# Further blocks of a mixture-of-experts kernel at 64 rows: high and low halves side by side in one stationary operand, woven into the first block's work

## Chip, cores and metric

One NeuronCore of a Trainium2 chip runs the whole program in one launch. The metric is the time on the device in microseconds (us); three executions of the kernel before are given, and their median stands for it. "PE" is the matmul engine, "ACT" the scalar engine, "DVE" the vector engine, "POOL" the general engine that also issues the indirect DMAs, and "SP" the engine that issues the other DMAs.

## The reference, cut to what matters

A decoder layer: forgetting attention, a residual with layer norm, and then a mixture of experts with 64 routed experts and one shared one. The change is in the mixture of experts. With T = 1024 tokens of width 1024 and an inner width of 256:

```python
scores = jax.nn.sigmoid((xf @ w_router).astype(jnp.float32))
...
_, top_e = lax.top_k(jnp.where(exp_mask, sel, -jnp.inf), TOP_K)   # 8 of 64 experts for each token
...
h = jax.nn.silu(xb @ w_gate[e]) * (xb @ w_up[e])
yb = (h @ w_down[e]) * rw[:, None].astype(xb.dtype)
return acc.at[rows].add(yb), None
...
shared = (jax.nn.silu(xf @ ws_gate) * (xf @ ws_up)) @ ws_down
```

So each expert has a list of the tokens that chose it. Computed from the reference on its own inputs, the 64 lists have 101 to 159 tokens, 128 on average. 33 experts have 128 tokens or fewer; 31 have more, and none of them over 159. Those 31 are experts 2-4, 6, 7, 9, 10, 15, 17, 19, 20, 22-27, 30, 31, 33-37, 39, 42, 44, 49, 51, 53 and 63. They form 16 runs, so 16 of them follow an expert without surplus (or the start) and 15 follow another one with surplus.

## The kernel before

The program first computes the attention (eight pairs of heads), then the output projection, layer norm and routing, token tile by token tile. DVE computes for each (token, expert) pair a place in a table (`place`), and POOL writes the token numbers into the table in DRAM (`list_tokens`). The table has `TAB_BLOCKS` = 8 columns per expert, each a block of up to 128 tokens.

Then come the blocks. A block is up to 128 rows of tokens and one expert's weights. The eight blocks of the shared expert (`SH` = 8) come first; then `expert(e, par)` is called for e = 0 to 63 on each of the engines, most of it in a loop over pairs of experts. Every operand of a matmul is held as two float32r parts, high and low, and a product is three matmuls: high by high, high by low, and low by high.

On PE a block has these parts:

- `turn_rows`: eight transposes of 128x128 that bring the gathered rows (`x_rows`) into a PSUM tensor, from which ACT copies the high part (`xb_hi`) and DVE subtracts the low part (`xb_lo`);
- `gate_up`: 24 matmuls with 512 moving columns into `banks[0]`: 16 with the high rows (against `gu_hi` and `gu_lo`) and 8 with the low rows;
- ACT takes the silu (`sg`), DVE multiplies (`hh`), and `turn_h` transposes the result (two transposes), ACT and DVE split it into `ht_hi` and `ht_lo`;
- `down`: 12 matmuls of 512 columns into `k_ps`, 8 with `ht_hi` and 4 with `ht_lo`; ACT scales the result by the token's weight into `ys` (`scale_rows`), and POOL adds it to a sum in DRAM (`scatter_add`, an indirect DMA).

An expert has a first block of up to 128 rows, and `further[e]` further blocks of up to 128 rows more; on these inputs that is 0 or 1. The order on PE inside `expert(e)` is: turn h of the block before; gate and up of the first block; if there is a further block, turn its rows into `out_ps`; turn the next expert's rows into `q_ps`; down of the block before; and then, if there is a further block, turn h of the first block, gate and up of the further block, and down of the first block. The further block's own h and down follow in the next expert.

The weights of one expert are three matrices of 1 MB. SP loads them into two raw buffers, ACT copies the high part (`w_high`, `L1166`, four pieces for gate and up and two for down), and DVE subtracts the low part (`w_low`, `L1546`), while the previous set is used.

POOL goes through its list in this order in `expert(e)`: wait until DVE has read the weights' column of the block (`w_ok`), gather the rows of expert e + 2; if expert e + 1 has a further block, gather its rows (`x_rows` 2, 128 rows of 4352 bytes); then add the results of expert e - 1 to the sums. A gather is a copy of 128 indices (`L575`) and then the indirect DMA (`L578`); an addition is the same with `L585` and `L588`.

Of the kernel before, what the change touches and what calls it, by code (L numbers as in the profile page):

```python
# [5 lines left out]
P = 128  # L6
BANK = 512
# [12 lines left out]
VC = 256  # L20
# [36 lines left out]
TAB_BLOCKS = T // P  # L57
# [16 lines left out]
def build(nc, x, w_in, b_f, w_out, ln1_g, ln1_b, router, router_bias, w_gate, w_up, w_down, ws_gate, ws_up,  # L74
          ws_down, ln2_g, ln2_b, out):
    with ExitStack() as ctx:
# [31 lines left out]
        with ExitStack() as early:  # L108
# [38 lines left out]
            with ExitStack() as d:  # L147
# [47 lines left out]
                pos_b = sb("pos_b", [P, E], c=d)  # L195
                dest = sb("dest", [P, E], c=d)
# [10 lines left out]
        with ExitStack() as m:  # L207
# [4 lines left out]
            xb_hi = [sb(f"xb_hi{i}", [P, DC, P], F32R, c=m) for i in range(3)]  # L212
            xb_lo = [sb(f"xb_lo{i}", [P, DC, P], F32R, c=m) for i in range(3)]
# [5 lines left out]
            wcol = [sb(f"wcol{i}", [P, 1], c=m) for i in range(3)]  # L219
# [23 lines left out]
        for n in ("consts masks xt_ps xt_hi_ok xt_lo_ok wf_in wf_ok bf_in zt_ps zt_ok z_ps z_ok zabs_ok zexp_ok zlog_ok zmin_ok gate_ok"  # L243
                  " c_ps c_hi_ok c_lo_ok c_stored wv_hi_ok wv_lo_ok v_ps v_ok aug aug0 mx20"
# [4 lines left out]
                  " g_hi_ok g_lo_ok d_hi_ok d_lo_ok tab_in started gated turned rows_hi_ok rows_lo_ok silu_ok h_ok ht_ps ht_hi_ok"  # L249
                  " ht_lo_ok downed scaled w_ok x_in x_turned x_rows_hi_ok x_rows_lo_ok x_w_ok ax_ok ax_stored summed"  # L250
                  " stands g2_in std_ok var_ok f_part set_free f_sum f_var f_std f_step f_mv f_norm f_g f_out").split():
            S[n] = sem(n)
        tile_in = [sem(f"tile_in{t}") for t in range(TT)]
        wv_in = [sem(f"wv_in{i}") for i in range(2)]
# [5 lines left out]
        wo_in = [sem(f"wo_in{i}") for i in range(STAGES)]  # L260
# [16 lines left out]
        S["sidx_ok"] = sem("sidx_ok")  # L277

# [42 lines left out]
        def _(sp):  # L321
# [3 lines left out]
            sp.dma_start(bf[:], b_f.to_broadcast([P, HEADS])).then_inc(S["bf_in"], 16)  # L325
            for n in range(NVC):
                if n >= 2:
                    sp.wait_ge(S["wv_lo_ok"], n - 1)
                sp.dma_start(wv[:, n % 2], w_rows[:, :, 2 * D + n * VC:2 * D + (n + 1) * VC]).then_inc(wv_in[n % 2], 16)
# [37 lines left out]
            for c in range(DC):  # L367
                if c >= STAGES:
                    sp.wait_ge(S["wo_lo_ok"], c - STAGES + 1)
                sp.dma_start(wo[:, c % STAGES], w_out[c * P:(c + 1) * P, :]).then_inc(wo_in[c % STAGES], 16)  # L370
# [80 lines left out]
            sp.dma_start(tab[:], tab_dram.rearrange("(p n) o -> p (n o)", p=P)).then_inc(S["tab_in"], 16)  # L451
# [26 lines left out]
            for t in range(TT):  # L478
                sp.wait_ge(S["f_part"], t + 1)
                load_sums(2, t)  # L480
                if t == 0:
                    sp.dma_start(g2[:], ln2_g.to_broadcast([P, D])).then_inc(S["g2_in"], 16)
                    sp.dma_start(b2[:], ln2_b.to_broadcast([P, D])).then_inc(S["g2_in"], 16)
# [6 lines left out]
        def _(pool):  # L490
# [81 lines left out]
            def gather(i, e, k, count, done):  # L572

                stand(pool)
                g.tensor_copy(gidx[i][:], tab[:, ds(e * TAB_BLOCKS + k, 1)]).then_inc(idx_ok[i], 1)  # L575
# [3 lines left out]
                                     in_offset=bass.IndirectOffsetOnAxis(ap=gidx[i][:, 0:1], axis=0)).then_inc(done, 16)  # L579

            def scatter_add(i, e, k, b, to):
                stand(pool)
                g.tensor_copy(sidx[i][:], tab[:, ds(e * TAB_BLOCKS + k, 1)]).then_inc(S["sidx_ok"], 1)  # L585
                pool.wait_ge(S["sidx_ok"], b - SH + 1)
# [4 lines left out]
            def add_first(par, e, b):  # L591

                pool.wait_ge(S["scaled"], b + 1)
                pool.wait_ge(sent[par], 8 * (e - par) + SENT_0[par])
                scatter_add(par, e, 0, b, par)

            def add_last_first(b, xi):

                pool.wait_ge(S["scaled"], b + 1)
                pool.wait_ge(sent[2], 16 * xi + SENT_0[2])  # L600
                scatter_add(1, E - 1, 0, b, 2)

# [1094 lines left out]
```

## Time and profile before

| what | value |
|---|---|
| median of the three executions | 2026.01 us |
| the three executions | 2014.58, 2026.01, 2034.15 us |
| the profiled execution, from its first to its last instruction | 2024.6 us |
| PE busy in it | 1834.1 us (91%) |
| DVE, ACT, POOL busy | 1169.8, 900.8, 471.2 us |
| mean granted PE clock, share of full | 0.954 |

The profile has no other time of the profiled execution than its span of 2024.6 us; it lies 1.4 us below the median, and inside the range of the three. The busy time of PE is made of matmuls whose ends are modelled, so the distance from one matmul's start to the next one's is read below, and not the length that a row gives. A part's period is the distance between the starts of two `turn_h` (`L949`), with which every block begins.

### The profile page before, as it was taken

The page shows a single profiled execution, that of the slowest core. Times are in us where ns is not written, and L with a number is a line of the kernel's source. Part 1 is how long each engine was busy: PE and PEld are TensorE (multiplying, and loading weights), DVE is VectorE, ACT ScalarE, POOL GpSimd, SP SyncE. Part 2 cuts the span into 40 slices and gives each one's busy share as a digit, 9 for nine tenths or more (in the row PEclk, how much of TensorE's full clock was granted, in tenths as well). Part 3 has the DMA queues.
Part 4 walks back from the last instruction along what each step waited for, and adds up shares of the span by engine and source line. Part 5 has one row for each costly group of instructions (what it writes and reads, how often), then busy time and mean ns, then how long its engine had stood idle before and what let it go on. Part 6 is the DMA issues. An engine that isn't in the chain of part 4 may idle for free.

```text
span 2024.6 us, 30936 instructions
## 1 busy us (share of the span) xinstructions
PE 1834.1 (91%) x8994; PEld 1469.5 (73%) x8995; DVE 1169.8 (58%) x1612; ACT 900.8 (44%) x1193; POOL 471.2 (23%) x517
## 2 busy tenths in 40 slices
PE   7998999999999979989899999999999999999910
PEld 5896777777777658767787877888778777777700
DVE  3102545644654678773656677655665677668737
ACT  3201322332231433333566677655665667668612
POOL 0020000000000022443233344333333334434303
PEclk9997999999999989889999999999999999999965
DMA  5221011101100244345989999999999999999882
GB/s 174 62 61 32 6 27 31 31 6 26 31 6 5 74 165 150 133 162 173 325 240 301 307 351 342 306 281 294 299 300 282 299 305 330 349 307 353 296 288 92
DMA packets 146255, 384.85 MB, mean 190 GB/s; under 512 B 33824, under 2 KB 58400, under 8 KB 146208
## 3 DMA queue, kind: packets, MB, share of 16 engines
q1 hardware_dynamic: 113840, 270.67, 37.2%
q0 software_dynamic: 32368, 113.56, 21.3%
q8 instruction: 28, 0.46, 0.1%
q14 instruction: 19, 0.16, 0.0%
HBM read 306.39 MB, written 77.79 MB: 190 GB/s over the span
## 4 chain that ended last, share of the span: by engine, by line
PE 66%; DMA 13%; DVE 7%; issue 6%; ACT 3%; POOLq 2%; ACTq 2%; POOL 1%; SPq 0%; another core or an unknown queue 0%; DVEq 0%
DMA x_rows<-rows_scratch,gidx 7%; PE out_ps L844 6%; PE bank L935 5%; PE bank L938 5%; PE bank L941 5%; PE bank L69 5%; PE bank L71 4%; PE bank L70 4%; PE k_ps L961 3%; PE k_ps L962 3%; PE k_ps L966 3%; DMA raw_gu<-in_moe_w_up_dram 3%; PE q_ps L71 2%; PE q_ps L69 2%; PE q_ps L925 2%
## 5 line engine op out<-in xcount | busy, mean ns | idle before, releaser
L935 PE MATMUL bank<-gu_hi,xb_hi 128*128 128x512 f32 x824 | 335.9, 408 | 4.1 <-DVE gu_lo L1546 2.7
L1546 DVE TENSOR_TENSOR gu_lo<-raw_gu,gu_hi 128x1024 fp32r<-128x1024 f32 x260 | 306.8, 1220 | 37.5 <-ACT gu_hi L1166 34.7
L938 PE MATMUL bank<-gu_lo,xb_hi 128*128 128x512 f32 x824 | 327.1, 397 | 0.0
L1166 ACT CAST gu_hi<-raw_gu 128x1024 fp32r<-128x1024 f32 x260 | 253.5, 1049 | 13.6 <-DMA raw_gu<-in_moe_w_gate_dram 8.8
L941 PE MATMUL bank<-gu_hi,xb_lo 128*128 128x512 f32 x824 | 209.0, 395 | 0.0
L935 PEld LDWEIGHTS bank<-gu_hi,xb_hi 128*128 128x128 f32 x824 | 156.8, 190 | 38.8 <-issue 2.1
L588 POOL DMA_INDIRECT sums_scratch<-ys,sidx x95 | 164.1, 1727 | 80.6 <-POOL sidx L585 70.7
L941 PEld LDWEIGHTS bank<-gu_hi,xb_lo 128*128 128x128 f32 x824 | 154.4, 187 | 37.8
L938 PEld LDWEIGHTS bank<-gu_lo,xb_hi 128*128 128x128 f32 x824 | 156.2, 190 | 33.2
L961 PE MATMUL k_ps<-dn_hi,ht_hi 128*128 128x512 f32 x412 | 172.0, 418 | 1.2 <-ACT ht_hi L1195 1.2
L1101 ACT ACTIVATE probs<-bank 128x512 f32<-128x512 f32 (+2 forms) x150 | 73.9, 505 | 209.8 <-PE bank L830 186.4
L962 PE MATMUL k_ps<-dn_lo,ht_hi 128*128 128x512 f32 x412 | 165.3, 401 | 0.0
L1546 DVE TENSOR_TENSOR dn_lo<-raw_dn,dn_hi 128x1024 fp32r<-128x1024 f32 x130 | 152.7, 1216 | 0.7 <-ACT dn_hi L1166 0.7
L1205 ACT ACTIVATE ys<-k_ps,wcol 128x1024 f32<-128x1024 f32 x95 | 106.5, 1121 | 93.4 <-PE k_ps L966 80.3
L1358 DVE TENSOR_REDUCE mx<-out_ps 128x1 f32<-128x512 f32 (+1 forms) x96 | 44.3, 488 | 179.4 <-PE out_ps L804 174.9
L1558 DVE TENSOR_TENSOR ht_lo<-bank,ht_hi 128x256 fp32r<-128x256 f32 x103 | 43.3, 420 | 179.1 <-ACT ht_hi L1195 177.0
L537 POOL IOTA e<- 128x64 f32 x1 | 0.2, 189 | 585.5 <-DVE xs L1376 585.5
L578 POOL DMA_INDIRECT x_rows<-rows_scratch,gidx x95 | 112.2, 1181 | 84.9 <-POOL gidx L575 79.2
L1166 ACT CAST dn_hi<-raw_dn 128x1024 fp32r<-128x1024 f32 x130 | 130.4, 1059 | 2.2 <-DMA raw_dn<-in_moe_w_down_dram 2.2
L844 PE MATMUL out_ps<-probs,va 128*128 128x512 f32 (+3 forms) x384 | 128.8, 489 | 0.4 <-ACT probs L1101 0.4
L575 POOL COPY gidx<-tab 128x1 int32 (+1 forms) x95 | 56.1, 591 | 286.8 <-DVE wcol L1564 263.8
L966 PE MATMUL k_ps<-dn_hi,ht_lo 128*128 128x512 f32 x412 | 113.1, 396 | 0.0
(268 smaller groups left out, 3824.0 us busy)
## 6 DMA issues: line engine op xcount, KB each, us to landing
raw_gu<-in_moe_w_gate_dram SPq DMA_DIRECT2D x128, 512.0 KB
raw_gu<-in_moe_w_up_dram SPq DMA_DIRECT2D x128, 512.0 KB
raw_dn<-in_moe_w_down_dram SPq DMA_DIRECT2D x128, 512.0 KB
wqk<-in_fox_w_in_dram SPq DMA_DIRECT2D x16, 512.0 KB, 5.2
fin<-sums_scratch SPq DMA_DIRECT2D x16, 512.0 KB, 10.4
sums_scratch<-zeros POOLq DMA_DIRECT2D x11, 512.0 KB, 8.0
xs<-in_x_dram SPq DMA_DIRECT2D x8, 512.0 KB, 7.0
wv<-in_fox_w_in_dram SPq DMA_DIRECT2D x4, 1024.0 KB, 7.1
```

What stands on the lines that cost most here:

```text
L69: pe.matmul(out, w_hi, m_hi, start=start, stop=False, skip_group_check=True)
L71: return pe.matmul(out, w_lo, m_hi, start=False, stop=stop, skip_group_check=True)
L588: g.indirect_dma_start(out=sums[to], out_offset=bass.IndirectOffsetOnAxis(ap=sidx[i][:, 0:1], axis=0), in_=ys[i][:], in_offset=None, compu ...
L844: i = pe.matmul(out_ps[:, q0:q0 + w], va[par][:, t, :], probs[:, at:at + w], start=t == 0, stop=t == (3 if q0 < BANK else TT - 1), skip_gr ...
L935: i = pe.matmul(o3, xb_hi[s][:, c], g_hi[:, :, c], start=c == 0, stop=False, skip_group_check=True)
L938: pe.matmul(o3, xb_hi[s][:, c], g_lo[:, :, c], start=False, stop=False, skip_group_check=True)
L941: i = pe.matmul(o3, xb_lo[s][:, c], g_hi[:, :, c], start=False, stop=c == DC - 1, skip_group_check=True)
L961: pe.matmul(k_ps[:, r], ht_hi[:, c], d_hi[:, c, r], start=c == 0, stop=False, skip_group_check=True)
L962: pe.matmul(k_ps[:, r], ht_hi[:, c], d_lo[:, c, r], start=False, stop=False, skip_group_check=True)
L966: i = pe.matmul(k_ps[:, r], ht_lo[:, c], d_hi[:, c, r], start=False, stop=c == FC - 1, skip_group_check=True)
L1166: a.copy(hi, raw).then_inc(S[done], 1)
L1546: dve.tensor_tensor(lo, raw, hi, ALU.subtract).then_inc(S[lo_ok], 1)
```

## The change

Further blocks now have at most 64 rows (`XR`), and the table has 1 + (1024 - 128) / 64 = 15 columns per expert, the first of 128 rows and the others of 64. On these inputs each of the 31 surplus experts still has exactly one further block.

The high and the low part of a further block's rows stand side by side in one tensor of 128 columns (`xo`): columns 0 to 63 high, 64 to 127 low. One pass with `gu_hi` and one with `gu_lo` then give, in PSUM partitions 0 to 63, the products of the high rows, and in 64 to 127 those of the low rows. ACT copies the lower partitions' half to `gu_x`, and DVE adds the two. The same is done for h (`ho`) and for the result: ACT copies partitions 64 to 127 of `out_ps` into `ys[2]` and DVE adds partitions 0 to 63. So a further block has 16 matmuls for gate and up instead of 24, and 8 for down instead of 12. The product low by low, which was left out before, is now added for these rows. The token's weight goes into h in `further_h` rather than into the result.

The order changes too. Inside an expert with a further block, all of that block now runs within its own expert, in the gaps of the first block's parts, and its rows are turned at the head of the expert. A first block's down is now always in the next expert. The accumulators of a further block are all in `out_ps`: the turned rows and gate and up in its two halves, and down over both, so its rows may be turned only when the further block before has left `out_ps` (`x_scaled`). On POOL the result of a further block is added within its own expert. Many semaphores are merged or renamed, which leaves the order of the attention part as it was.

The core of the diff:

```diff
-TAB_BLOCKS = T // P
+XR = P // 2
+XR_BITS = XR.bit_length() - 1
+TAB_BLOCKS = 1 + (T - P) // XR
...
+            def gather_further(e, k, x):
...
+                g.indirect_dma_start(out=xg[2][0:XR], out_offset=None, in_=rows_dram,
+                                     in_offset=bass.IndirectOffsetOnAxis(ap=gidx[2][0:XR, 0:1], axis=0)).then_inc(S["x_in"], 16)
...
                     with pool.If(f1 > 0):
-
                         pool.wait_ge(S["x_w_ok"], xi + nx + 1)
-                        gather(2, e + 1, 1, xi + nx, S["x_in"])
-                with pool.If(nx < 2):
-                    left_over()
...
+                        gather_further(e + 1, 0, xi + nx)
...
+                else:
+                    add_first(1 - par, e - 1)
+                with pool.If(nx > 0):
+                    add_further(e, nx - 1, xi + nx - 1)
...
+            def turn_further(x):
+
+                pe.wait_ge(S["x_in"], 16 * x + 16)
+                pe.wait_ge(S["x_scaled"], x + 1)
...
+            def gate_up_further(w, x):
...
+                pe.wait_ge(S["x_rows_lo_ok"], x + 1)
+                for c in range(DC):
+                    pe.matmul(o3, xo[:, c], g_hi[:, :, c], start=c == 0, stop=False, skip_group_check=True)
+                    i = pe.matmul(o3, xo[:, c], g_lo[:, :, c], start=False, stop=c == DC - 1, skip_group_check=True)
...
+            def turn_h_further(x):
+                pe.wait_ge(S["x_h_ok"], x + 1)
...
+            def down_further(w, nset, x):
+                d_hi, d_lo = split[w][2:4]
+                pe.wait_ge(S["x_ht_lo_ok"], x + 1)
+                pe.wait_ge(S["d_lo_ok"], D_PIECES * nset)
...
                 with pe.If(nx > 0):
...
+                    turn_further(xi)
+                    turn_h(m - 1)
+                    pe.wait_ge(S["g_lo_ok"], G_PIECES * (e + 2))
+                    gate_up(par, w, "rows_", m + 1)
+                    gate_up_further(w, xi)
+                    turn_next()
+                    down_hi(m - 1, par, e + 1)
+                    turn_h_further(xi)
+                    down_lo(m - 1, par)
+                    down_further(w, e + 2, xi)
...
+                    further_rows_hi(xi)
+                    h_hi(m - 1)
+                    if pos != "last":
+                        next_gate_up(m, e, par)
+                    silu(m)
+                    further_half(xi)
+                    if pos != "last":
+                        rows_hi(1 - par, q_ps, "turned", m + 2, "rows_hi_ok")
+                    further_silu(xi)
+                    down_weights()
+                    further_h_hi(xi)
+                    rows_before()
+                    further_y_half(xi)
...
+                    further_sum(xi)
+                    next_rows()
+                    further_h(xi)
+                    down_weights()
+                    further_h_lo(xi)
+                    further_y(xi)
```

Two places show how instructions move. On PE, between the first block's gate and up and the next expert's rows, before (`x_rows` into `out_ps` are the further block's rows, into `q_ps` the next expert's):

```order
L941 MATMUL bank<-gu_hi,xb_lo 128x512 x8
L1013 REGISTER_ALU
L1013 TENSOR_LOAD further
L1013 ISA x2
L1014 COMPARE_AND_BRANCH
L1015 ISA
L925 MATMUL out_ps<-ident,x_rows 128x128 x8
L1014 UNCONDITIONAL_BRANCH
L1018 ISA
L925 MATMUL q_ps<-ident,x_rows 128x128 x8
```

On PE at the head of an expert after the change, up to the first matmul of the first block's gate and up:

```order
L1044 TENSOR_LOAD further
L1044 ISA x2
L1051 COMPARE_AND_BRANCH
L970 ISA
L971 REGISTER_ALU
L975 MATMUL out_ps<-ident,x_rows 128x64 x8
L937 REGISTER_ALU
L940 MATMUL bank<-ident,hh 128x128 x2
L1054 ISA
L924 REGISTER_ALU
L926 MATMUL bank<-gu_hi,xb_hi 128x512
```

The eight transposes of the further rows moved from behind the first block's gate and up to ahead of it and of `turn_h`; they have 64 columns now.

On DVE in an expert with a further block, from that block's rows on, before:

```order
L1550 TENSOR_TENSOR xb_lo<-out_ps,xb_hi 128x1024
L1616 UNCONDITIONAL_BRANCH
L1546 TENSOR_TENSOR gu_lo<-raw_gu,gu_hi 128x1024
L1550 TENSOR_TENSOR xb_lo<-q_ps,xb_hi 128x1024
L1546 TENSOR_TENSOR dn_lo<-raw_dn,dn_hi 128x1024 x2
L1623 COMPARE_AND_BRANCH
L1558 TENSOR_TENSOR ht_lo<-bank,ht_hi 128x256
L1564 COPY wcol<-x_rows 128x1
L1553 REGISTER_ALU
L1554 TENSOR_TENSOR hh<-sg,bank 128x256
```

On DVE in such an expert after the change, from the first block's product on (`gu_x`, `ho` and `ys` are the further block's):

```order
L1624 TENSOR_TENSOR hh<-sg,bank 128x256
L1616 TENSOR_TENSOR gu_lo<-raw_gu,gu_hi 128x1024
L1644 TENSOR_TENSOR gu_x<-out_ps,gu_x 64x512
L1620 TENSOR_TENSOR xb_lo<-q_ps,xb_hi 128x1024
L1648 SCALAR_TENSOR_TENSOR gu_x<-gu_x,w_x 64x256
L1616 TENSOR_TENSOR dn_lo<-raw_dn,dn_hi 128x1024 x2
L1653 TENSOR_TENSOR ho<-bank,ho 128x2x64
L1658 TENSOR_TENSOR ys<-out_ps,ys 64x1024
```

The further block's four steps on DVE now stand between the next expert's rows and the weights for down, one behind each, and the last step follows the split of the weights.

## Rows read from the trace of the kernel before

**Rows 1.** The page: the span, and DMA share in 40 equal slices

```profile
span 2024.6 us, 30936 instructions
...
DMA  5221011101100244345989999999999999999882
```

**Rows 2.** PE timeline: turn_h that opens expert 0, and the last one after expert 63

```profile
966.78 0.39 PE L949 MATMUL bank<-ident,hh 128*128 128x128 f32 x2
...
1925.56 0.39 PE L949 MATMUL bank<-ident,hh 128*128 128x128 f32 x2
```

**Rows 3.** PE timeline: expert 18 (1240.70), 19 with further block (1250.22, 1262.02), 20 (1270.65)

```profile
1240.70 0.39 PE L949 MATMUL bank<-ident,hh 128*128 128x128 f32 x2
...
1250.22 0.39 PE L949 MATMUL bank<-ident,hh 128*128 128x128 f32 x2
...
1257.32 1.16 PE L925 MATMUL out_ps<-ident,x_rows 128*128 128x128 f32 x8 [1.12 <-DMA x_rows<-rows_scratch,gidx]
...
1262.02 0.39 PE L949 MATMUL bank<-ident,hh 128*128 128x128 f32 x2
...
1262.71 0.39 PE L935 MATMUL bank<-gu_hi,xb_hi 128*128 128x512 f32 x1
...
1265.98 2.03 PE L941 MATMUL bank<-gu_hi,xb_lo 128*128 128x512 f32 x8
...
1270.65 0.39 PE L949 MATMUL bank<-ident,hh 128*128 128x128 f32 x2
```

**Rows 4.** Waits in 966 to 1925 us: total, times, longest

```profile
PEld out_ps L925 <- DMA x_rows<-rows_scratch,gidx: 35.7, 14, 6.2
...
PE out_ps L925 <- DMA x_rows<-rows_scratch,gidx: 29.6, 14, 5.8
```

**Rows 5.** Stretches: us, busy of PE, PEld, DVE, ACT, POOL, clock, DMA share, GB/s

```profile
966.80:1925.60 958.80, 918.64 (x4364) 753.94 (x4363) 624.23 (x759) 614.22 (x759) 348.59 (x374) 0.99 0.96 309
...
1872.00:1906.00 34.00, 30.18 (x138) 23.65 (x138) 26.69 (x31) 25.11 (x31) 11.33 (x12) 1.00 1.03 371
```

**Rows 6.** Instruction groups: count, busy us, mean ns of one, idle before

```profile
L588 POOL DMA_INDIRECT sums_scratch<-ys,sidx x95 | 164.1, 1727 | 80.6 <-POOL sidx L585 70.7 <-DVE wcol L1564 6.4 <-issue 3.6
...
L1550 DVE TENSOR_TENSOR xb_lo<-q_ps,xb_hi 128x1024 fp32r<-128x1024 f32 x72 | 87.7, 1218 | 18.2 <-ACT xb_hi L1187 18.2
...
L1187 ACT CAST xb_hi<-q_ps 128x1024 fp32r<-128x1024 f32 x72 | 73.3, 1018 | 30.7 <-PE q_ps L925 27.6 <-remote 2.3 <-issue 0.7
...
L1558 DVE TENSOR_TENSOR ht_lo<-bank,ht_hi 128x256 fp32r<-128x256 f32 x103 | 43.3, 420 | 179.1 <-ACT ht_hi L1195 177.0 <-issue 2.1
...
L1079 ACT COPY v_out<-bank 128x512 f32<-128x512 f32 x16 | 9.4, 586 | 76.2 <-PE bank L71 69.0 <-DMA v_scratch<-v_out 7.2
...
L1203 ACT COPY ys<-k_ps 128x1024 f32<-128x1024 f32 x8 | 8.1, 1014 | 14.1 <-PE k_ps L966 12.2 <-remote 1.9
...
L1310 DVE TENSOR_TENSOR xt_lo<-bank,xt_hi 128x512 fp32r<-128x512 f32 x6 | 3.9, 683 | 10.7 <-ACT xt_hi L1049 10.7
```

**Rows 7.** POOL timeline in expert 18: gathers for expert 20 and for 19's further block

```profile
1245.73 1.23 POOL L578 DMA_INDIRECT x_rows<-rows_scratch,gidx  x1 [0.89 <-POOL gidx L575]
...
1249.27 1.42 POOL L578 DMA_INDIRECT x_rows<-rows_scratch,gidx  x1 [0.87 <-POOL gidx L575]
```

**Rows 8.** PE timeline: expert 30, its further rows and the next expert's

```profile
1434.10 0.39 PE L949 MATMUL bank<-ident,hh 128*128 128x128 f32 x2
1443.89 1.97 PE L925 MATMUL out_ps<-ident,x_rows 128*128 128x128 f32 x8 [3.80 <-DMA x_rows<-rows_scratch,gidx]
1445.65 1.89 PE L925 MATMUL q_ps<-ident,x_rows 128*128 128x128 f32 x8
```

**Rows 9.** PE timeline: expert 2 and its further block, the first of all

```profile
985.82 0.39 PE L949 MATMUL bank<-ident,hh 128*128 128x128 f32 x2
1005.06 0.39 PE L949 MATMUL bank<-ident,hh 128*128 128x128 f32 x2
```

**Rows 10.** PE timeline: experts 61 and 62, in a run of nine without surplus

```profile
1883.57 0.50 PE L949 MATMUL bank<-ident,hh 128*128 128x128 f32 x2 [0.62 <-DVE hh L1554]
1894.98 0.50 PE L949 MATMUL bank<-ident,hh 128*128 128x128 f32 x2 [0.64 <-DVE hh L1554]
```

More of the change, by code:

```diff
@@ L950, in turn_h, with down_hi @@
                 i.then_inc(S["ht_ps"], 1)
-            def down(b, w, nset):
+            HALVES = [slice(half * BANK, (half + 1) * BANK) for half in range(2)]
+            def down_hi(b, w, nset):
                 d_hi, d_lo = split[w][2:4]
@@ L957, in down @@
                     pe.wait_ge(S["scaled"], b)
[L958 to L959 removed]
+                for r in HALVES:
                     for c in range(FC):
@@ L1014, in expert @@
                 with pe.If(nx > 0):
-                    pe.wait_ge(S["x_in"], 16 * xi + 16)
-                    turn_rows(xg[2], out_ps).then_inc(S["x_turned"], 1)
-                if not last:
-                    pe.wait_ge(got[1 - par], 8 * (e + par) + 16)
-                    turn_rows(xg[1 - par], q_ps).then_inc(S["turned"], 1)
-                down(b0 - 1, par, e + 1)
-                with pe.If(nx > 0):
-                    turn_h(b0)
-                    gate_up(2, w, "x_rows_", xi + 1)
-                    down(b0, w, e + 2)
+                    turn_further(xi)
@@ L1035, in _ @@
+                with pe.If(nx < 1):
+                    turn_h(m - 1)
+                    pe.wait_ge(S["g_lo_ok"], G_PIECES * (e + 2))
+                    gate_up(par, w, "rows_", m + 1)
+                    turn_next()
+                    down(m - 1, par, e + 1)
             with pe.Fori(0, E // 2 - 1) as i:
@@ L1038, in _ @@
             expert(E - 2, 0)
-            b0, nx = expert(E - 1, 1, last=True)
-            turn_h(b0 + nx)
-            down(b0 + nx, 0, E + 1)
+            expert(E - 1, 1, last=True)
+            turn_h(SH + E - 1)
+            down(SH + E - 1, 0, E + 1)
         @block.scalar
@@ new lines, in expert @@
+                            further_silu(xi + k)
+                            further_h_hi(xi + k)
+                            further_y_half(xi + k)
+                with act.If(nx < 1):
+                    h_hi(m - 1)
+                    if pos != "last":
+                        next_gate_up(m, e, par)
+                    silu(m)
+                    if pos != "last":
+                        rows_hi(1 - par, q_ps, "turned", m + 2, "rows_hi_ok")
+                    down_weights()
+                    rows_before()
```

396 lines of the change are left out of this document (219 added, 177 removed).

## The prediction, made blind

> **What bounds the kernel now.** I read the page first, then the PE timeline of the experts, then the waits and the stretches, and last POOL's own timeline.
>
> The page shows a span of 2024.6 us, and DMA engines that are nine tenths busy or more from the middle on [rows 1]. That second half is the experts. They run from the `turn_h` at 966.78 us to the one at 1925.56 us, which is 958.8 us [rows 2], with PE granted 0.99 of its clock and the DMA at 309 GB/s [rows 5]. Nothing ahead of the experts changes by more than a few small DVE instructions, so the sum is made on these 958.8 us.
>
> Expert 18, which has no surplus ("plain"), takes 1240.70 to 1250.22, 9.52 us. The further block of expert 19 takes 1262.02 to 1270.65, 8.63 us, and the turn of its rows (0.89 us, the difference of the two) stands in its first block's period, so it costs 9.52 us too [rows 3]. 95 blocks at 9.52 us are 904.4 us. The other 54.4 us are waits. Nearly all of them are one wait: the further block's rows are late. PE's two parts sat idle for them 14 times each, 29.6 and 35.7 us, up to 6.2 us [rows 4]. The reader should see that every case is a further block behind a plain expert; behind another surplus expert the rows are in time.
>
> In a long run of plain experts the DMA takes over: expert 61 takes 11.41 us instead of 9.52 [rows 10], with the DMA share at 1.03 and 371 GB/s [rows 5]. The weights are 3.15 MB an expert and the two indirect DMAs 1.08 MB; 4.23 MB at 371 GB/s are 11.4 us. That run costs about 9 us over its 9.52 us periods.
>
> **Instructions removed.** The distance of two matmuls of 512 columns is 0.2336 us: 14 of them from 1262.71 to 1265.98 [rows 3]. A further block loses 8 + 4 of them, 2.80 us. Its ten transposes have 64 moving columns instead of 128. Eight cost 0.89 us now. Halved, ten would save 0.5 us; at the least they save nothing. I take 0.2, nearer to nothing, because the weight loads between them keep their 128 columns. A surplus expert then has 19.04 - 3.0 = 16.0 us of PE work, and over 31 of them 93 us are at stake.
>
> On this the Trainium skill has a rule ("TensorE: Matmul & The Clock Gate", section on LDWEIGHTS): a weight load costs by its columns and not by the rows it contracts. By it the transposes save nothing, and the sum below would be 6 us higher.
>
> **The further block's chain, woven in.** Each of its parts is now queued in order on ACT and DVE behind first-block work. I add up one surplus expert from its first transpose. From one engine to the next I put 0.03 us between ACT and DVE and 0.2 behind a matmul. PE: rows turned to 0.8; `turn_h` to 0.95; gate and up of the first block to 6.65; 16 matmuls of the further block to 10.4; next rows to 11.3; eight matmuls of the first down to 13.2. Then `turn_h_further` needs h of the further block. ACT copies the half at 10.6 (0.59, as 128x512 of L1079) to 11.2; DVE adds (0.68, as L1310) to 11.9. But ACT then has the next rows (from 11.45, 1.02) to 12.5 ahead of the silu, and DVE their low part (1.22) to 13.7 ahead of the product, which takes 0.42 to 14.1 [rows 6]. PE waits from 13.2 to 14.2: 1.0 us. Then comes the transpose and the four low matmuls to 15.3. `down_further` needs the low part of h, and on DVE the split of the down weights (two of 1.13) stands ahead of it: 14.1 to 16.4, and 0.3 more to 16.7. PE waits to 16.8: 1.5 us. Eight matmuls end at 18.7. So the surplus expert takes 18.7 us instead of 19.04; 31 of them 579.7 us. If the copies of 64 partitions or fewer columns were much shorter than their rows it would be 18.0; with 0.7 us more of overhead between the engines, 19.4.
>
> **The new wait on `out_ps`.** When the next expert has a surplus too, its rows may be turned only after ACT has copied the upper half of the result (0.2, then 1.01 as L1203) and DVE has added the lower (1.2): 2.6 us with PE's restart, before which nothing of that expert can run, since this turn is now its first instruction. 15 experts follow another with surplus: 39 us (33 to 44).
>
> **The gather, needed earlier.** This is the largest term. Behind a plain expert the rows of a further block are turned 16.6 us after that expert's start (1257.32 against 1240.70), and this is already late, by 1.4 us. The change needs them at 9.5 us, at the head of the surplus expert, 7.1 us earlier than they come. POOL does not send for them earlier. It now adds the result of the further block of expert e - 1 at its end, 2.4 us into expert e, and only then comes the gather for e + 2: copy 0.2, wait 0.85, issue 1.7 (L588), and it starts at about 6.4 us instead of at 5.0 (1245.73) [rows 3, 6, 7], which is 1.3 later. Against that, the further gather has 64 rows instead of 128 and the DMA has fewer bytes in a longer time. From the end of the issue (1250.69) to PE are 6.6 us now; I take 4.5, and 0.8 less in the two issues. So PE waits 7.1 + 1.3 - 2.1 - 0.8 = 5.5 us. With the gather as quick as half of 6.6 it would be 4.3; with nothing gained, 8.4. What is queued behind this wait is all of PE's work of the expert, and with it ACT and DVE.
>
> A long gap has a price of its own. After PE's gap in expert 30 the two turns took 1.97 and 1.89 us where they take 1.05 or so in the other rows, at 1.2 instead of 2.4 GHz; the distance of their starts is 1.76 instead of 0.89 [rows 8]. Some 1.7 us were lost there; I take 1.0 on average, and 6.5 us for a wait in all. 14 such cases are 91 us; expert 2, late by 8.8 us already (two turns and 36 matmuls, 10.4 us, took 19.24 [rows 9]) and needed 6 us earlier, makes 15, and expert 63, whose gather has no wait for `w_ok` ahead, 2: together 108 us, where there were 54 us less the 9 of the run.
>
> The Trainium skill says otherwise of such a gather ("DMA: Bandwidth & Descriptors", section "Anatomy of one DMA — SWDGE (gpsimd) path"): about 2.0 us plus the bytes at 436 GB/s, here 2.6 us for 64 rows. The 6.6 us of the trace stand against it, with all DMA engines busy; by the rule the sum is that of the second rival.
>
> **Sum.** 33 plain experts at 9.52: 314.2. 31 surplus experts at 18.7: 579.7. `out_ps`: 39. Late rows: 108. The DMA's long run: 9. Together 1050 us instead of 958.8: 91 us more. The longer table (480 KB instead of 256 to write and to read) and one more link in DVE's `place` add some 2 us. 2024.6 + 93 = 2118 us for an execution like the profiled one, which lies 1.4 us below the median of the three.
>
> **Rivals.**
> *The work counts (faster).* If the chain hides on ACT and DVE and the gather is in time as often as now, the 93 us of PE work come off and the 54 us of waits stay: 1932 us. It decides if the waits in a surplus expert stay under 3.0 us in all. For it: ACT and DVE are busy only two thirds of the stretch [rows 5]. Against it: the order on both engines is fixed, and the sum of their queues gives the waits, however idle they are elsewhere. The DMA's 11.4 us in plain experts would hold it nearer to 1945.
> *Only the gather is quick.* With 2.6 us from issue to PE, the wait behind a plain expert is 3.6 us and the clock stays: 14 x 3.6 + 13 = 63 instead of 108, 2073 us.
> *Nearly even.* Chain as in the sum, but late rows cost no more than now (54): 2055 to 2065 us; with short copies as well, near 2035.
> *The clock too.* If each gap halves the clock for most of the first block's gate and up (5.7 us at full speed), each of the 16 cases costs 3 us more: about 2165 us.
>
> **How the numbers follow.** The sum, 2085 to 2160: 0.55. Only the gather quick, 2045 to 2085: 0.22. Nearly even, within 1% of now: 0.07. The work counts: 0.11. The clock, over 2160: 0.05. A measurement of this kernel can tell about 1%, 20 us. Faster by more: 0.11; within: 0.07; slower: 0.82. The faster case and a part of the even one are left out below and the clock's above: 2042 to 2160. By the lowest bounds of all terms (31 x 18.0, 33, 14 x 4.3) the experts take 987 us and the kernel 2055.
>
> **What would show it.** Right: PE waiting at the head of a surplus expert behind a plain one for `x_rows` for some 5 us, 16 times; 2 to 3 us behind a surplus one for DVE's last step; two waits of 1 to 1.5 us inside, for DVE's product and for the low part of h; a period of 18 to 19 us; a DMA share well under 0.9; clock lapses behind the gaps. Wrong: a surplus expert near 16 us, or rows that land in time, or POOL's gather for the further block starting well ahead of 8 us into the plain expert.

## The result, and the profile after

| | kernel before | changed kernel |
|---|---|---|
| median, same chip, 4 runs each | 2028.95 us (2014.58 to 2034.15) | 2259.15 us (2249.01 to 2265.94) |
| ratio, 95% interval | 1 | 1.1135 (1.1089 to 1.118) |
| span of the profiled execution | 2024.6 us | 2247.1 us |
| mean granted PE clock | 0.954 | 0.901 |
| first to last `turn_h` of the experts | 958.8 us | 1183.4 us |

The median of the kernel before is now that of four executions, with one of 2031.88 us beside the three known ahead. The change makes the kernel 11.4% slower. The direction was right; 2118 us was 141 us too low, and the range ended at 2160. Of the 222.5 us that the span grew, 224.6 lie in the experts, so nothing ahead of them matters.

The page of the changed kernel: each digit of the clock row is one fortieth of the span, in tenths of full speed.

```profile
span 2247.1 us, 29232 instructions
...
PEclk9998999999999988988889888889898889889965
DMA  5120110101002625486878977778776778979963
```

The second half shows clock digits of 8, and a DMA that is no longer full: both say that PE stands still often. The stretch of the experts (us, then busy of PE, PEld, DVE, ACT, POOL, granted clock, DMA share, GB/s) answers to [rows 5]:

```profile
964.60:2148.00 1183.40, 933.80 (x3991) 734.94 (x3990) 662.56 (x820) 626.38 (x790) 342.73 (x374) 0.88 0.80 236
```

A clock of 0.88 instead of 0.99 is half speed (1.2 instead of 2.4 GHz) for 0.24 of the stretch, 280 us. Which waits there are, in 964 to 2150 us (engine, tile and line, who ended the wait: total, times, longest), answers to [rows 4]:

```profile
PE out_ps L975 <- DMA x_rows<-rows_scratch,gidx: 134.9, 16, 12.9
...
PE out_ps L975 <- DVE ys L1658: 37.8, 15, 2.5
...
PE bank L993 <- DVE gu_x L1648: 30.2, 31, 1.0
...
PE out_ps L1002 <- DVE ho L1653: 28.9, 31, 1.4
```

These are the four waits that were forecast, at the places forecast, 16, 15, 31 and 31 times. A surplus expert behind a surplus expert shows three of them in its PE timeline:

```profile
1696.61 1.11 PE L975 MATMUL out_ps<-ident,x_rows 64*128 64x64 f32 x8 [2.52 <-DVE ys L1658]
1697.65 0.70 PE L940 MATMUL bank<-ident,hh 128*128 128x128 f32 x2
1698.00 0.77 PE L926 MATMUL bank<-gu_hi,xb_hi 128*128 128x512 f32 x1
1698.58 0.63 PE L929 MATMUL bank<-gu_lo,xb_hi 128*128 128x512 f32 x1
1699.00 0.63 PE L926 MATMUL bank<-gu_hi,xb_hi 128*128 128x512 f32 x1
...
1703.02 2.03 PE L932 MATMUL bank<-gu_hi,xb_lo 128*128 128x512 f32 x8
...
1712.52 0.42 PE L993 MATMUL bank<-ident,gu_x 64*128 64x64 f32 x2 [0.98 <-DVE gu_x L1648]
...
1714.98 0.50 PE L1002 MATMUL out_ps<-dn_hi,ho 128*128 128x512 f32 x1 [0.92 <-DVE ho L1653]
...
1719.63 1.07 PE L975 MATMUL out_ps<-ident,x_rows 64*128 64x64 f32 x8 [2.52 <-DVE ys L1658]
```

From 1696.61 to the next turn, at 1719.63, it is 23.0 us. The starts from 1698.58 to 1699.00 are 0.42 us apart instead of 0.2336: behind a wait of only 2.52 us PE works at 1.2 GHz. From `turn_h` to the low-row matmuls it takes 5.37 us (1697.65 to 1703.02) where 0.25 and 16 matmuls are 3.99: 1.4 us are lost. Without them the expert would be 21.6 us; 21.3 (18.7 and 2.6) were forecast.

A surplus expert behind a plain one waits for its rows. PE's rows, the plain expert's `turn_h` first:

```profile
1741.70 0.39 PE L940 MATMUL bank<-ident,hh 128*128 128x128 f32 x2
...
1760.42 1.12 PE L975 MATMUL out_ps<-ident,x_rows 64*128 64x64 f32 x8 [9.06 <-DMA x_rows<-rows_scratch,gidx]
1761.47 0.70 PE L940 MATMUL bank<-ident,hh 128*128 128x128 f32 x2
```

and POOL's in the same place, which answer to [rows 7] (L618 adds the previous further block's result, L585 gathers for expert e + 2, L594 is the gather in question):

```profile
1745.69 1.44 POOL L618 DMA_INDIRECT sums_scratch<-ys,sidx  x1 [0.80 <-POOL sidx L615]
1746.77 0.97 POOL L582 COPY gidx<-tab 128x1 int32 x1
1748.63 1.10 POOL L585 DMA_INDIRECT x_rows<-rows_scratch,gidx  x1 [0.89 <-POOL gidx L582]
1751.09 0.38 POOL L591 COPY gidx<-tab 64x1 int32 x1 [1.36 <-issue]
1752.33 0.94 POOL L594 DMA_INDIRECT x_rows<-rows_scratch,gidx  x1 [0.85 <-POOL gidx L591]
```

The issue ends at 1753.27, 11.6 us into the plain expert (10.5 forecast), and PE starts 7.15 us later (4.5 forecast). So the wait is 9.06 us and not 5.5. In the other late cases but expert 2's (5.6 us) the second distance is 6.5 to 8.5 us.

### The profile page after: what moved, and what is told of

Same layout as the page of the kernel before. It is cut to its first block, busy times and chain, and to the rows that moved or that the text cites. A ratio compares the mean times of both kernels' runs of the same rounds, so it can differ in the third digit from the quotient of the medians.

```text
span 2247.1 us, 29232 instructions
## 1 busy us (share of the span) xinstructions
PE 1848.9 (82%) x8622; PEld 1451.3 (65%) x8623; DVE 1211.7 (54%) x1690; ACT 913.1 (41%) x1224; POOL 464.9 (21%) x517
## 4 chain that ended last, share of the span: by engine, by line
PE 59%; DVE 12%; DMA 10%; issue 8%; ACT 5%; POOL 2%; POOLq 2%; DVEq 1%; another core or an unknown queue 0%; SPq 0%; ACTq 0%
DMA x_rows<-rows_scratch,gidx 7%; PE out_ps L835 6%; PE bank L926 5%; PE bank L929 5%; PE bank L71 4%; PE bank L73 4%; PE bank L72 4%; PE bank L932 4%; DVE dn_lo L1616 3%; PE out_ps L985 3%; PE out_ps L984 3%; PE q_ps L916 2%; PE out_ps L1002 2%; PE q_ps L71 2%; PE q_ps L72 2%
## 5 line engine op out<-in xcount | busy, mean ns | idle before, releaser
L926 PE MATMUL bank<-gu_hi,xb_hi 128*128 128x512 f32 x576 | 267.2, 464 | 1.3 <-ACT ex L1198 1.3
L929 PE MATMUL bank<-gu_lo,xb_hi 128*128 128x512 f32 x576 | 256.0, 444 | 0.0
L975 PE MATMUL out_ps<-ident,x_rows 64*128 64x64 f32 x248 | 34.2, 300 | 172.7 <-DMA x_rows<-rows_scratch,gidx 134.9
L932 PE MATMUL bank<-gu_hi,xb_lo 128*128 128x512 f32 x576 | 146.1, 395 | 0.0
L932 PEld LDWEIGHTS bank<-gu_hi,xb_lo 128*128 128x128 f32 x576 | 108.0, 187 | 26.4
L602 POOL DMA_INDIRECT sums_scratch<-ys,sidx x64 | 111.5, 1742 | 56.4 <-POOL sidx L599 47.0
L953 PE MATMUL k_ps<-dn_hi,ht_hi 128*128 128x512 f32 x288 | 121.2, 421 | 1.4 <-ACT ht_hi L1235 1.4
L954 PE MATMUL k_ps<-dn_lo,ht_hi 128*128 128x512 f32 x288 | 114.8, 399 | 0.0
L1620 DVE TENSOR_TENSOR xb_lo<-q_ps,xb_hi 128x1024 fp32r<-128x1024 f32 x72 | 88.0, 1222 | 42.2 <-ACT xb_hi L1227 41.1
L1658 DVE TENSOR_TENSOR ys<-out_ps,ys 64x1024 f32<-64x1024 f32 x31 | 37.7, 1217 | 134.0 <-ACT ys L1304 134.0
```

What stands on the lines that cost most here:

```text
L602: g.indirect_dma_start(out=sums[to], out_offset=bass.IndirectOffsetOnAxis(ap=sidx[i][:, 0:1], axis=0), in_=ys[i][:], in_offset=None, compu ...
L926: i = pe.matmul(o3, xb_hi[s][:, c], g_hi[:, :, c], start=c == 0, stop=False, skip_group_check=True)
L929: pe.matmul(o3, xb_hi[s][:, c], g_lo[:, :, c], start=False, stop=False, skip_group_check=True)
L932: i = pe.matmul(o3, xb_lo[s][:, c], g_hi[:, :, c], start=False, stop=c == DC - 1, skip_group_check=True)
L953: pe.matmul(k_ps[:, r], ht_hi[:, c], d_hi[:, c, r], start=c == 0, stop=False, skip_group_check=True)
L954: pe.matmul(k_ps[:, r], ht_hi[:, c], d_lo[:, c, r], start=False, stop=False, skip_group_check=True)
```

## The experiments

The theory: the work saved is real, but four waits and the half clock behind them cost several times as much. The rivals: one of these causes is the whole of it; the clock has a cause other than PE's own waits; or the two passes cost as much as they save. The runs were made on three chips, on which the kernel before takes 2018.5 us (the first four runs), 2019.6 us (the next four) and 2020.8 us (the last two). Each ratio is against the kernel before on the same chip, and a time is the median of 4 runs (10 for the last). The changed kernel was timed where the kernel before took 2028.95 us, and its ratio is 1.1135; so gains over it are told as differences of ratios, with 0.01 at about 20 us. Every edit is to the changed kernel unless the text says otherwise, and the edits are shown condensed.

**The gather, one expert earlier.**

```diff
 if f1 > 0:                      # expert e + 1 has a further block
-    gather_further(e + 1, 0, xi + nx)
+    if nx > 0: gather_further(e + 1, 0, xi + nx)
+if f1 < 1 and further_of(e + 2) > 0:
+    gather_further(e + 2, 0, xi + nx)
```

> Changed kernel, but POOL sends for a further block's rows one expert earlier whenever the expert in between has no surplus. Theory A (waits at three places, and the clock that lapses behind each gap): the 16 waits of about 9 us for the gathered rows go, 16 x 9 = 144 us, and the lapses behind them with them, some 30 us more: 2259 - 174 = 2085 us. Theory B (the DMA engines are the limit, so that rows land late however early they are sent for): over 2220 us. Theory C (the two-pass further block is itself slower than the three-pass one): 2115 us or so, the waits' 144 us only, with the periods of surplus experts unchanged.

Measured: 2082.04 us, ratio 1.030 (1.026 to 1.035). PE's waits in its experts:

```profile
PE out_ps L986 <- DVE ys L1669: 37.8, 15, 2.5
PE bank L1004 <- DVE gu_x L1659: 30.1, 31, 1.0
PE out_ps L1013 <- DVE ho L1664: 28.8, 31, 1.4
...
PE out_ps L986 <- DMA x_rows<-rows_scratch,gidx: 4.1, 2, 3.4
```

The wait for rows is gone (134.9 to 4.1 us) and the others stand to a tenth of a microsecond. In ratio this is 0.083 of the time, 168 us: more than the 131 us of waits, since part of the half clock went as well (it costs 56 us in this profile instead of 100, counted as in the table below). That is theory A. C, with the waits' 144 us alone, and B are out. It is the largest cause, but the kernel is still slower than before.

**The chain, ahead of the first block's work.** On ACT the down weights' high parts move ahead of the further block's half, and its silu ahead of the next rows; on DVE

```diff
+down_weights()
 further_sum(xi)
-next_rows()
 further_h(xi)
-down_weights()
 further_h_lo(xi)
+next_rows()
 further_y(xi)
```

> Changed kernel, but on ACT and DVE the split of the down weights stands ahead of the further block's half and sum, and the next expert's rows behind the further block's silu, product and low part of h. Theory A: the two waits inside a surplus expert, 1.0 + 1.4 us with PE's restarts, go in all 31: 2259 - 78 = 2181 us, and 2155 if lapses of the clock go with them. Theory B (down weights arrive from DRAM too late to be split earlier): ACT and DVE wait for them ahead of the further block, 2240 us or more.

Measured: 2140.94 us, ratio 1.060 (1.055 to 1.066). Both inner waits are gone from PE's list but for one of 0.6 us; the waits for rows stay at 128.2 us. By ratio 107 us are gained: 59 are the waits, 7 stand at the late rows, and 37 are the clock (the half clock costs 63 us in this profile instead of 100); 4 stay open. Where it went can be seen: `down_further`, behind the second inner wait, ran at distances of 0.43 us in 19 of the 31 surplus experts, and does so in none now. So A holds. The time lies 14 us below its range, of which 11 are the chip, on which the kernel before is faster too.

**The turn, between the high and the low half of the first block's gate and up.**

```diff
-turn_further(xi)
 turn_h(m - 1)
-gate_up(par, w, "rows_", m + 1)
+gate_up(par, w, "rows_", m + 1, lambda: turn_further(xi))
```

with the two steps on its rows moved behind `h` on ACT and behind three of the four weight splits on DVE.

> Changed kernel, but the further rows are turned 3.9 us later, between the 16 high and the 8 low matmuls of the first block's gate and up (and their split on ACT and DVE behind the weights of gate and up). Theory A: the wait of 2.6 us for out_ps goes in 15 experts, 39 us, the waits for gathered rows become 3.9 us shorter in 16, 62 us, and 30 us of lapses: about 2130 us. Theory C (the further block's own work is what became slow): at most 10 us gained.

Measured: 2148.22 us, ratio 1.062 (1.057 to 1.067). The 37.8 us behind `ys` go, 22.9 us for the low part of the rows come (the split stands ahead of it), and the waits for rows fall from 134.9 to 69.9 us, since the turn now comes 4 us later. The gain by ratio is 104 us where A had 129, without the new wait; C, at most 10 us, is out:

```profile
PE out_ps L977 <- DMA x_rows<-rows_scratch,gidx: 69.9, 15, 8.8
...
PE out_ps L986 <- DVE xo L1639: 22.9, 15, 1.8
```

**PE kept busy, nothing else changed.** 24 transposes of the identity, which nothing reads, ahead of the turn in each surplus expert.

```diff
+for _ in range(24):
+    pe.transpose(banks[1][:, FF + P:FF + 2 * P], ident[:], ident[:])
 turn_further(xi)
```

> Changed kernel with 24 more transposes of the identity (2.7 us at full clock, into a part of PSUM that nothing reads) at the head of each surplus expert, where PE waits anyway for out_ps or for gathered rows. Theory A (the clock lapses because PE idles there): they cost nothing, and the lapses behind the waits for out_ps go: the period of a surplus expert behind a surplus one falls from 23 to 25 us to about 21.5 us, 15 x 2 = 30 us less, 2230 us; low-clock time falls from 280 us by 50 or more. Theory D (the lapses come from the 64-row operands or from the chip's load): low-clock time stays near 280 us and the time at 2259 us or more.

Measured: 2223.39 us, ratio 1.104 (1.096 to 1.113). With 744 more matmuls on PE the kernel is not slower, and faster by 0.009 in ratio, though the two intervals overlap. The profile is plainer. Its stretch of the experts, from the `turn_h` of expert 1 on:

```profile
965.00:2121.60 1156.60, 976.88 (x4689) 788.00 (x4689) 655.79 (x812) 616.41 (x781) 342.36 (x371) 0.93 0.80 238
```

The clock is 0.93 instead of 0.88. All experts together, from 953.3 to 2121.6 us, take 1168.3 us instead of 1183.4, while the DMA share is the same 0.80 and the rows land no sooner behind their issue (6.3 to 7.9 us). PE is at half clock for 171 us instead of 280, which costs 66 us instead of 100; the experts are only 15 us shorter, so the filler, or something beside it, took some 20 us back. D, with the half clock at 280 us, is out: part of it at least comes of PE's own idle time and has no cause outside. Beside the filler PE still waits 95.2 us for late rows, and the half clock stays there.

**Pairs, and all three.** The same edits combined: first the gather and the chain, then the gather and the turn, then all.

> The changed kernel with the early gather and the moved chain, the turn of the further rows still first in its expert. Theory A: against the early gather alone (2082) the two inner waits of 30 and 29 us go, and with them the half clock behind them: 1990 to 2015 us, with the 38 us of waits for DVE's last step left. Theory B (the chain's gain of 118 us beside late rows was owed to the late rows, since an expert that ends earlier only waits longer, or to chance): under 40 us, 2045 us or more.

Measured: 1990.97 us, ratio 0.987 (0.984 to 0.990), as in A.

> The changed kernel with the early gather and the later turn of the further rows, the chain as it was. Theory A: against the early gather alone (2082) the 38 us of waits for DVE's last step go, the inner waits of 59 us and most of the half clock stay, and a wait of 20 us for the low part of the further rows comes: 2045 to 2070 us. Theory B (the turn's place does not matter once the rows are there, the lost time moves to the inner waits): 2075 to 2090 us.

Measured: 2061.79 us, ratio 1.021 (1.019 to 1.024). The turn's place, worth 0.052 (104 us) alone, is worth 0.009 (18 us) once the gather is early: most of what it gave alone was more time for the late rows. The chain is worth 0.053 alone and 0.043 beside the early gather (87 us). The time lies in the range of A.

> All three edits in one kernel: the further gather one expert earlier, the further block's steps ahead of the down weights and the next rows on ACT and DVE, and its turn between the high and the low half of the first block's gate and up. Theory A (the work saved is real, and it was covered by waits and by the clock that they cost): no wait at the head of a surplus expert, none of over 1 us inside; a surplus expert is 16 us, a plain one between 9.52 and the DMA's 11.4 us. 31 x 16 + 33 x 9.5 to 11.4 are 810 to 872 us where the kernel before takes 953 on this chip: 1880 to 1940 us, faster than the kernel before by 4 to 7%. Theory B (a rival: two passes with one stationary operand of 128 columns, 64-partition steps and one more block woven in cost as much as they save, on DVE or on the DMA): the surplus expert stays at 18 us or more, 1990 to 2030 us.

Measured: 1958.08 us, ratio 0.969 (0.968 to 0.971). That is faster than the kernel before by 3.1%, and the best of all kernels here, but 18 us above the range of A: of the waits A is right, and of the length of a surplus expert B. Beside the two others the turn's place is worth 0.018 (36 us). Alone the three edits give 0.188 in sum, together 0.144. The stretch of the experts from the `turn_h` of expert 1 on, and one surplus expert in it:

```profile
972.00:1858.40 886.40, 849.24 (x3945) 667.43 (x3946) 656.20 (x810) 617.78 (x779) 364.86 (x367) 1.00 0.98 309
1325.41:1343.66 18.25, 17.43 (x81) 13.35 (x81) 12.22 (x16) 11.69 (x16) 7.61 (x8) 1.00 0.89 239
```

And from the PE timeline of this expert, the two turns, the transposes of its h and the waits:

```profile
1329.58 1.09 PE L988 MATMUL out_ps<-ident,x_rows 64*128 64x64 f32 x8
1330.60 2.13 PE L945 MATMUL bank<-gu_hi,xb_lo 128*128 128x512 f32 x8
1333.06 0.50 PE L997 MATMUL out_ps<-gu_hi,xo 128*128 128x512 f32 x1 [0.33 <-DVE xo L1650]
...
1339.74 0.45 PE L1006 MATMUL bank<-ident,gu_x 64*128 64x64 f32 x2
1340.12 1.20 PE L974 MATMUL k_ps<-dn_hi,ht_lo 128*128 128x512 f32 x4
...
1343.66 0.50 PE L953 MATMUL bank<-ident,hh 128*128 128x128 f32 x2 [0.49 <-issue]
```

The clock is whole again, with the same 64-row operands, so they are not what lowered it, and PE idles for 0.82 us of 18.25. (Ahead of this stretch, in front of expert 1's `turn_h`, PE stands still for 5.67 us, and for 4.25 us in the changed kernel; the profile names nothing that it waits for, and the kernel before has no such gap. With expert 0 the experts take 901.6 us.) But the expert is not 16.0 us. The ten transposes take 1.02 and 0.38 us (differences of the starts, up to the next matmul): 1.40 where I had 0.94. The rest is handovers between kinds of matmul, some 0.1 us each (0.32 us from 1337.71, the first matmul behind a turn, to the next start instead of 0.2336), of which the woven order has four or five more, and the two short waits. Full-clock work is 17.1 us: 18.25, less 0.5 around the wait for `xo` and 0.65 at the end.

**The kernel before, with the early gather alone.** The same edit on the kernel before.

> The kernel before with nothing changed but that the gather for a further block behind a plain expert is issued one expert earlier. Theory A (late rows are all that stands between the kernel before and 9.52 us a block, apart from the DMA): the 54 us of waits fall to 10 to 25, 1975 to 1995 us. Theory B (the DMA is then the bound, its share is 0.96 already): the time saved comes back in waits for weights, 2005 to 2020 us. The difference between this kernel and the one with all three edits is what two passes at 64 rows are worth: A 50 to 90 us.

Measured: 2006.93 us, ratio 0.995 (0.993 to 0.996). PE's waits in its experts:

```profile
PE q_ps L935 <- DMA x_rows<-rows_scratch,gidx: 23.4, 7, 7.3
```

The wait at `out_ps` is gone (29.6 in [rows 4]), but the first blocks' rows, which were waited for 5.1 us before, are now late by 23.4, up to 7.3 us at a time. So it is neither A nor B, though the time lies in B's range: not the weights are late, but another gather. A surplus expert is 19.04 us here (10.42 and 8.62, 31 times less a few), and 18.25 with the two passes and the weave: 0.8 x 31 = 25 of the 49 us between this kernel and the one with all three edits. Of the rest 17 are this wait, 6.0 us there; what is left was not separated.

**The gather for the further rows ahead of that for e + 2**, in plain experts, to see what the distance from issue to PE depends on.

```diff
+if nx < 1 and f1 > 0: gather_further(e + 1, 0, xi + nx)
 gather(par, e + 2, (e + 2 - par) // 2)
-if f1 > 0: gather_further(e + 1, 0, xi + nx)
+if nx > 0 and f1 > 0: gather_further(e + 1, 0, xi + nx)
```

> The changed kernel, and on POOL in a plain expert the gather for the next expert's further rows is issued ahead of the gather for expert e + 2 instead of behind it. In the row at 1752.33 it then starts at about 1748.6, 3.7 us earlier. Theory A (from the end of the issue to PE it is 7.1 us whatever stands ahead of it, since the weights keep the DMA engines busy): the waits for x_rows fall from about 9 to about 5.4 us each, 16 times, 59 us, with some of the half clock behind them: 2175 to 2205 us. Theory B (half of the 7.1 us was the queue behind the gather for e + 2, so that my 4.5 us would have held with the queue empty): 6.3 us less each, 2130 to 2160 us. Theory C (the gather for e + 2 is now late in its turn): 2210 us or more, with waits for x_rows at q_ps.

Measured: 2205.81 us, ratio 1.096 (1.088 to 1.104). One case, on POOL and on PE:

```profile
1579.98 1.05 POOL L594 DMA_INDIRECT x_rows<-rows_scratch,gidx  x1 [0.89 <-POOL gidx L591]
```

The turn that it serves:

```profile
1589.50 1.11 PE L981 MATMUL out_ps<-ident,x_rows 64*128 64x64 f32 x8 [6.50 <-DMA x_rows<-rows_scratch,gidx]
```

From the end of the issue (1581.03) it is 8.5 us, and 6.7 to 8.8 in the other late cases. So the gather ahead of it on POOL is not what makes it slow, and B falls. But A is not met either: PE's waits for `x_rows` sum to 102.6 us instead of 134.9, 32 us less where A had 59, since the distance is 7.8 us on average in the 15 cases, against 7.2 in the changed kernel.

The DMA packets show where the time goes, in one case each. In this one the first packet of 4352 bytes starts at 1584.08, 3.1 us after the end of the issue, and the last of the 64 at 1588.0. In the changed kernel (issue to 1753.27) the first starts at 1756.27, 3.0 us after it, and the 64 starts take 2.6 us. In the kernel before, a gather of 128 rows (issue to 1250.69) starts at 1253.87, 3.2 us after it, and its 128 starts take 2.6 us as well. So half the rows saved nothing, neither ahead of the first packet nor in the packets. What makes it slow (the weights on the same DMA engines, or the writing of its descriptors) was not separated.

**One pass run once more**, in the kernel with all three edits: 8 matmuls of 512 columns per further block, whose result is overwritten.

```diff
+for c in range(8):
+    pe.matmul(o3, xo[:, c], g_hi[:, :, c], start=c == 0, stop=c == 7)
 for c in range(DC):
```

> The kernel with all three edits, and in each further block one of the passes of gate and up (8 matmuls of 512 columns) run once more ahead of the others, its result overwritten. 31 x 8 x 0.2336 us are 58 us more PE work, two thirds of what the change removes. Theory A (PE bounds the surplus experts once their waits are gone, so work removed from them is worth its full length): 1958 + 58, 2005 to 2020 us, no faster than the kernel before with the early gather (2007). Theory B (the DMA, at a share of 1.02 to 1.04 in most blocks, or DVE's queue sets their time, and PE's work is partly beside it): 1965 to 1990 us, and what two passes gave was only in part the work.

Measured: 2022.16 us (10 runs), ratio 1.0015 (0.9986 to 1.0045). It costs 64 us (0.032 in ratio), and in the profiles the experts take 957.7 us instead of 901.6, 56 more, where the matmuls alone are 58. So A, though 2 us above its range: PE bounds the surplus experts, and a matmul removed from them is worth all of its length, although the DMA share of the experts is 0.97 without the pass and 0.93 with it. With two thirds of the saving put back, the kernel is no faster than before.

## Why the prediction was right in direction and short in size

In the terms of the sum, with the full-clock work of a surplus expert from the kernel with all three edits and the waits from the changed kernel's own list:

| term | forecast | measured | difference |
|---|---|---|---|
| work: 33 x 9.52, and 31 surplus experts | 31 x 16.0 | 31 x 17.1 | +34 |
| the two inner waits (with 0.2 of change-over) | 84 | 59 | -25 |
| the wait for `out_ps` | 39 | 38 | -1 |
| the wait for the late rows | 94 | 135 | +41 |
| half clock | 14 | about 100 | +86 |
| DMA in the long run; measured: what is left of the sum | 9 | about 7 | -2 |
| sum | 1050 | 1183 | +133 |

The half clock's cost is half of the distances between matmul starts (those under 0.7 us) in the pieces at 1.2 GHz: 100 us out of 280 in 52 pieces; the rest of these pieces are waits. The last row holds 4.25 us of the gap ahead of expert 1, which was not forecast.

- **Right: the four waits**, their places, how often each comes, and the order of the queues on ACT and DVE that makes them. The period of a surplus expert behind a surplus one at full clock (21.6 against 21.3) and the `out_ps` wait (2.52 against 2.6 with PE's restart) came out as summed.
- **Right: that the gather is the first cause.** Moved alone it gives back 0.083, 168 us. But the step "I take 4.5" for the time from the end of the issue to PE failed: it is 7.15, and 6.5 to 8.5 in others. The trace of before had 6.6 us for 128 rows [rows 4, 7]; I took off 2.1 for fewer bytes, and nothing came off. The Trainium skill ("DMA: Bandwidth & Descriptors", section "Anatomy of one DMA — SWDGE (gpsimd) path") gives an estimate of 2.6 us; the measurement decides against it here. Smaller errors on POOL: the gather for e + 2 began 0.5 us later than forecast; between it and the next copy lie 1.36 us in which the engine waits for nothing, 1.03 in the kernel before (ahead of the copy at 1247.99), from where they were carried over; and the two issues are 0.6 us shorter, not 0.8. Of the term for late rows, 14 cases were to wait 5.5 us each and waited 9.0, 126.6 us in all. Against that, expert 2 was priced at 15 us and waited 4.7 (expert 63: 2 and 3.6), so the 41 us in the table hide an error of 50.
- **Wrong: the price of the clock.** This is the step that missed by most, 86 us. "I take 1.0 on average" was said for the late rows only. Expert 30 [rows 8] was the only lapse I had looked at; it followed 3.80 us, and I took gaps of 2.5 us for free. Here such a gap is followed by six matmuls at 1.2 GHz, and the wait of 9.06 us by the two of `turn_h` and nine more. The rival "the clock too" had the mechanism, but 48 us for it, 16 times, and 0.05 of the chances. It comes at all 31 heads (from `turn_h` to the low-row matmuls 5.1 to 6.2 us, 31 times, instead of 3.99; 51 us in all), and in 19 experts also behind the second inner wait (29 us in all): a period of 24.8 us, in which `down_further` ran at distances of 0.43 us, alternates with that of 23.0. The Trainium skill ("TensorE: Matmul & The Clock Gate", section "HAM oscillation — how this bites in real kernels") tells of the same pattern: a kernel that waits for a DMA between bursts of matmuls, and starts each burst at the low clock. The trace agrees at the late rows, and shows it behind waits of 2.52 us for DVE too.
- **Wrong: 16.0 us of work.** The 2.80 us of removed matmuls are real (the run with one pass more prices 8 of them, 1.87 us by their distances, at 1.8 by the profiles and 2.1 by the times), but the ten transposes of 64 columns became dearer, not cheaper, and the weave adds handovers. In the kernel with all three edits the first and the last of eight such transposes start 0.82 us apart, where those of 128 columns have 0.78; and from the last one to the next matmul it is 0.20 us instead of 0.03. So most of what they cost more is the handover behind them. The tile view of `x_rows` after the change has the weight loads (min, median, max of one, in ns):

```profile
L916 PEld LDWEIGHTS q_ps<-ident,x_rows x576: 185/192/231, 868.8 to 2120.6; 128*128 128x128 f32 x192
...
L975 PEld LDWEIGHTS out_ps<-ident,x_rows x248: 182/202/206, 995.3 to 2128.1; 64*128 64x128 f32 x124
```

  The operand loaded has 128 columns either way, and takes 202 ns with 64 rows where it takes 192 with 128, as in the kernel with all three edits at full clock. That fits with nothing being saved; why the handover is longer stays open.
- **The inner waits were over-priced** (31 x 2.7 against 59), and hid the error in the work: the two nearly cancel in a surplus expert's period, so that its closeness to the forecast is luck. The first wait came as summed (0.98 us against 1.0), the second, for the low part of h, is 0.93 us and not 1.5.
- **A misread row of before.** The prediction calls nearly all of the 54.4 us of waits late rows. PE's own idle time for them is 29.6 us; the 35.7 us of its weight loads run beside it and do not add. The half clock, counted as above, cost the kernel before another 8 us. (And in the sum of one surplus expert `turn_h` ends at 1.05 us and not at 0.95; the times behind it are right.)
- **"The work counts"** was rightly unlikely for this kernel, and its condition, waits under 3.0 us in a surplus expert and rows in time as often as now, did not hold. With the three edits it does hold, and the kernel comes to 1958 us; the rival's "nearer to 1945" was close.

## What to carry to other kernels

Put the first instruction of a block where its operand has long landed: a wait at the head of a queue in order cost its own length here and then the matmuls behind it at half clock, so price a wait in a matmul stream with the clock that it costs (here 100 us on 232 us of waits). Take the time from a gather's issue to its use from the trace, and do not scale it with the bytes while the DMA is busy. Of causes that stand one behind another, what each is worth alone does not add up (the turn's place: 104 us alone, 18 beside the early gather, 36 beside both others), so test the pairs before choosing which to mend.

## What I had not expected of the hardware

- PE fell to 1.2 GHz behind waits of 2.52 us, in a stream whose other gaps in the 20 us ahead were of 1 us; distances of 0.42 us instead of 0.2336 show it. In the kernel with all three edits, whose waits are 0.3 to 0.5 us in the surplus expert shown, the stretch has a clock of 1.00.
- Eight transposes of 64 columns, with 64 rows loaded, take 1.02 us up to the next matmul, and eight of 128 columns 0.81 (1336.90 to 1337.71 in the kernel with all three edits). 0.17 of the difference lies between the last transpose and the next matmul.
- A gather of 64 rows was no quicker than one of 128: some 3 us from the end of the issue to the first packet and 2.6 us for the packets' starts, in one case of each.
- 24 transposes that nothing reads, in each surplus expert, did not lengthen the kernel (1.104 against 1.1135) and brought the clock of the experts from 0.88 to 0.93.
- An earlier gather for one block made that of another late (5.1 to 23.4 us in the kernel before).
